# Memory turned by DMA in 2-byte halves instead of by sixteen TensorE transposes, in a two-block transformer kernel

## The reference, cut to what matters

```python
mn = rms_norm_2(mem, norm_mem[l])            # mem: (1, 256, 1024), gain of 1024
xkv = (mn @ xa_w_kv[l]).reshape(b, mem.shape[1], 2, XA_HEADS, XA_HEAD_DIM)
xk = rms_norm_2(xkv[:, :, 0], xa_k_norm[l])
xv = xkv[:, :, 1]
```

## Time and profile before

| | |
|---|---|
| median of 3 runs | 959.49 us (959.39 to 959.93) |
| the profiled execution | 959.49 us, span 957.7 us |
| PE busy | 952.7 us, 99% of the span |
| DVE, ACT, POOL busy | 698.4, 537.6, 125.9 us |
| granted TensorE clock | 1.000 over the whole span |
| HBM traffic | 179 GB/s over the span |

### The profile page before, as it was taken

One profiled execution on the slowest core, in us unless ns is written; L12 is line 12 of the kernel. 1 busy time (PEld: TensorE's weight loads), 2 busy tenths in 40 slices (PEclk: granted clock), 3 DMA queues, 4 the chain that ended last, 5 costly groups with the idle time before them and its releaser, 6 DMA issues.

```text
span 957.7 us, 20451 instructions
## 1 busy us (share of the span) xinstructions
PE 952.7 (99%) x8266; PEld 938.1 (98%) x8266; DVE 698.4 (73%) x1090; ACT 537.6 (56%) x783; POOL 125.9 (13%) x87
## 2 busy tenths in 40 slices
PE   9999999999999999999999999999999999999998
PEld 8999999999999999999999999999999999999998
DVE  5677657477879968877776656688698898887752
ACT  7454454356558964455545465587576674545531
POOL 0111110010036100002111112310002021223100
PEclk9999999999999999999999999999999999999999
DMA  8865675555454454575666665355245355655761
GB/s 264 253 210 176 188 252 167 185 176 179 152 194 140 141 168 133 177 263 176 193 201 198 222 202 178 95 159 175 89 139 172 131 177 174 211 187 177 254 208 65
DMA packets 169167, 172.42 MB, mean 180 GB/s; under 512 B 5748, under 2 KB 167054, under 8 KB 168974
## 3 DMA queue, kind: packets, MB, share of 16 engines
q1 hardware_dynamic: 168270, 170.70, 55.4%
q10 hardware_dynamic: 832, 0.79, 0.3%
HBM read 170.42 MB, written 1.06 MB: 179 GB/s over the span
## 4 chain that ended last, share of the span: by engine, by line
PE 99%; DMA 1%; SPq 0%; DVE 0%; issue 0%; ACT 0%
PE acc L798 87%; PE part L848 1%; PE acc L848 1%; PE part L890 1%; PE part L914 1%; DMA xraw<-in_x 1%; PE part L1204 1%; PE part L900 1%; PE acc L671 1%; PE part L1194 0%; PE part L1227 0%; PE part L1013 0%; PE part L1406 0%; PE part L936 0%; PE part L1214 0%; PE part L1260 0%
## 5 line engine op out<-in xcount | busy, mean ns | idle before, releaser
L464 ACT ACTIVATE wh<-raw 128x1024 fp32r<-128x1024 f32 (+2 forms) x291 | 316.4, 1112 | 269.0 <-PE acc L798 119.2
L483 DVE TENSOR_TENSOR wl<-raw,wh 128x1024 fp32r<-128x1024 f32 (+2 forms) x292 | 393.1, 1385 | 47.2 <-ACT wh L464 46.6
L798 PE MATMUL acc<-ah,wh 128*128 128x256 f32 x1504 | 415.0, 279 | 0.0
L798 PE MATMUL acc<-al,wh 128*128 128x256 f32 x1504 | 409.1, 276 | 0.0
L798 PE MATMUL acc<-ah,wl 128*128 128x256 f32 x1496 | 406.2, 277 | 0.0
L798 PEld LDWEIGHTS acc<-ah,wh 128*128 128x128 f32 x1504 | 282.0, 188 | 3.3 <-issue 2.5
L798 PEld LDWEIGHTS acc<-al,wh 128*128 128x128 f32 x1504 | 280.4, 188 | 0.0
L798 PEld LDWEIGHTS acc<-ah,wl 128*128 128x128 f32 x1496 | 278.0, 188 | 0.1
L798 PE MATMUL acc<-hh,wh 128*128 128x256 f32 x352 | 97.3, 277 | 0.0
L798 PE MATMUL acc<-hh,wl 128*128 128x256 f32 x352 | 97.2, 276 | 0.0
L798 PE MATMUL acc<-hl,wh 128*128 128x256 f32 x352 | 97.2, 276 | 0.0
(11 more groups left out here) (476 smaller groups left out, 1557.2 us busy)
## 6 DMA issues: line engine op xcount, KB each, us to landing
raw<-in_ffn_w_down SPq DMA_DIRECT2D x24, 1408.0 KB, 6.4
raw<-in_w_in SPq DMA_DIRECT2D x33, 1024.0 KB, 5.3
raw<-in_ffn_w_gate SPq DMA_DIRECT2D x32, 1024.0 KB, 5.3
raw<-in_ffn_w_up SPq DMA_DIRECT2D x32, 1024.0 KB, 5.4
raw<-in_w_out SPq DMA_DIRECT2D x8, 1024.0 KB, 5.2
raw<-in_w_proj_attn SPq DMA_DIRECT2D x4, 1024.0 KB, 5.2
raw<-in_w_proj_mlstm SPq DMA_DIRECT2D x4, 1024.0 KB, 5.5
raw<-in_xa_w_kv SPq DMA_DIRECT2D x4, 1024.0 KB, 5.2
```

What stands on the lines that cost most here:

```text
L464: nc.scalar.activation(wh[:, slot, a * nw:b * nw], raw[:, slot, a * nw:b * nw], ACT.Copy).then_inc(S("w_hi"), 1)
L483: nc.vector.tensor_tensor(wl[:, slot, a * nw:b * nw], raw[:, slot, a * nw:b * nw], f(wh[:, slot, a * nw:b * nw]), SUB).then_inc(S("w_lo"), 1)
L798: ins = mm(dst, a, b, start=st and q == 0, stop=en_ and q == sweep[-1], skip_group_check=True)
```

## The change

The memory's transposing leaves TensorE. VectorE copies `memraw` into two planes of 2-byte halves (`mem_planes`: all low halves, all high halves). ScalarE issues four transposing DMAs, one for each half and block of 128 tokens, each over 128 x 1024 elements of two bytes, into `mem_turned`. VectorE then puts the halves together again with two copies, over `memraw`, which now holds `memT` (channels on partitions). `mo` and `mlo` are computed from there instead of from PSUM. The unread 32x256 product after the transposes is gone too. The two new tiles lie in the room of `mo` and `mlo`, which are written later. The diff, without the changes in the list of semaphores:

```diff
@@ sbuf
+        with ExitStack() as sc:
+            mem_planes = sb("mem_planes", [P, 2, TB, D], u16, scope=sc)
+            mem_turned = sb("mem_turned", [P, 2, DC, T], u16, scope=sc)
...
+        mem_halves = memraw[:, :, :].bitcast(u16).rearrange("p b (c h) -> p b h c", h=2)
+        memT = memraw[:, :, :].rearrange("p b c -> p (b c)").rearrange("p (k t) -> p k t", k=DC)
+        memT_halves = memraw[:, :, :].bitcast(u16).rearrange("p b c -> p (b c)").rearrange("p (k t h) -> p h k t", k=DC, h=2)
@@ TensorE
-                                narrow=(1, Q[0]) if (st, q, r) in (("n1", 0, 1), ("n3", 1, 0)) else None)
+                                narrow=(1, Q[0]) if (st, q, r) == ("n1", 0, 1) else None)
...
-            def memory_in(q, r):
-                if (q, r) == (0, 1):
-                    pe.wait_ge(*signal("mem_in", 16))
-                    transpose_in(memraw, "mem_ps", Q[2:6])
-
-            feed_forward("f2u", "f2d", "n3", between=memory_in)
+            feed_forward("f2u", "f2d", "n3")
@@ ScalarE, memory_hi
+                    act.wait_ge(*signal("mem_pl", 1))
+                    for h in range(2):
+                        for b in range(TB):
+                            act.dma_start_transpose(mem_turned[:, h, :, b * P:(b + 1) * P], mem_planes[:, h, b, :]).then_inc(S("mem_tr"), 16)
                 elif q < 3:
+                    act.wait_ge(*signal("mem_T", 1))
                     for j in (2 * q - 2, 2 * q - 1):
-                        act.wait_ge(*signal("mem_ps", j + 1))
                         for c in range(2):
-                            ins = A_(mo[:, 2 * j + c, :], Q[2 + j][:, c * T:(c + 1) * T], ACT.Copy, scale=col(V_MEM + 2 * j + c))
+                            ins = A_(mo[:, 2 * j + c, :], memT[:, 2 * j + c, :], ACT.Copy, scale=col(V_MEM + 2 * j + c))
@@ VectorE, feed_forward and memory_lo
                 looped(dve, FP, body, peel=2 if conv else 1)
+                if st == "n3":
+                    between(-1)
...
-                if q == 0:
+                if q < 0:
+                    dve.wait_ge(*signal("mem_in", 16))
+                    for b in range(TB):
+                        ins = V.tensor_copy(mem_planes[:, :, b, :], mem_halves[:, b, :, :])
+                    ins.then_inc(S("mem_pl"), 1)
+                elif q == 0:
                     dve.wait_ge(*signal("mem_sq", 2))
+                    dve.wait_ge(S("mem_tr"), 64)
+                    for h in range(2):
+                        ins = V.tensor_copy(memT_halves[:, h, :, :], mem_turned[:, h, :, :])
+                    ins.then_inc(S("mem_T"), 1)
                     V.tensor_scalar(e7[:, :], ms7[:, 0:2], EPS, EPS, ADD, MUL).then_inc(S("e7"), 1)
```

More of the change, by code:

```diff
@@ L89, in shared_signals @@
     chains = {
-        "mixer2_dve": [("e7", 1), ("mem_lo", 4), ("kpe", 1), ("la_lo", 1), ("rho2", 1), ("kv_e", 1), ("kv_rd", 1), ("akv", 1),
+        "mixer2_dve": [("mem_pl", 1), ("mem_T", 1), ("e7", 1), ("mem_lo", 4), ("kpe", 1), ("la_lo", 1), ("rho2", 1), ("kv_e", 1), ("kv_rd", 1), ("akv", 1),
                        ("rho7", 1), ("k_ss", 4), ("k_ms", 1), ("eq", 1), ("kt", 1), ("qt", 1), ("gl_cum", 2),
@@ L96, in shared_signals @@
                        ("sog", 1), ("gl_sq", 2), ("gl_sd", 1), ("xf_sd", 1)],
-        "mixer2_pe": [("mem_ps", 4), ("kv_ps", 1), ("uk_ps", 3), ("gl_z", 1), ("uq_ps", 3), ("kq_T", 8),
+        "mixer2_pe": [("kv_ps", 1), ("uk_ps", 3), ("gl_z", 1), ("uq_ps", 3), ("kq_T", 8),
                       ("gl_keT", 1), ("gl_att", 1), ("gl_dS", 3), ("gl_o", 2), ("go_T", 2), ("xq_ss", 2)],
@@ L232, in build @@
         rin = sb("rin", [P, 2, 4])
+        u16 = mybir.dt.uint16
         ah = sb("ah", [P, DC, T], f32r)
@@ L2517, in memory_lo @@
                             k = 2 * j + c
-                            ins = V.scalar_tensor_tensor(mlo[:, k, :], Q[2 + j][:, c * T:(c + 1) * T], col(V_MEM + k), f(mo[:, k, :]), MUL, SUB)
+                            ins = V.scalar_tensor_tensor(mlo[:, k, :], memT[:, k, :], col(V_MEM + k), f(mo[:, k, :]), MUL, SUB)
                         ins.then_inc(S("mem_lo"), 1)
```

## The result

The changed kernel takes 962.97 us (median of 6 runs, 962.49 to 964.73) where the kernel before takes 959.50: a ratio of 1.0037, 95% interval 1.0024 to 1.0050. It is slower by 3.5 us. The time lies in the predicted range, on the predicted side, and 2.0 us above the predicted 961.0.

A forecast was written before the change was run, and what follows sets the result against it. TensorE's stream was taken as the bound (PE busy 952.7 of 957.7 us); from 959.49 us, 1.9 saved and 3.4 waited on ScalarE's issues gave +1.5, 961.0 us, range 957.2 to 975.

The forecast's parts named there:

- What TensorE saves: At slab 2's start, 16 transposes, a slow first step and an unread product leave TensorE: 1.9 us less.
- VectorE's copies: Four copies of 2048 two-byte elements per partition, 1.3 us each; first pair from 558.66 to 561.3, mostly in idle time.
- X: Time of one transposing issue on ScalarE: bounds 0.373 and 2.98 us, middle 1.73 taken.
- The wait on ScalarE: Four issues delay ScalarE's split of slab 2, so TensorE waits 4X - 3.5 us before slab 2: 3.4 us.
- The wait on VectorE: VectorE waits for all four DMAs before its merging copies and slab 3's low part: cost nothing, 0.6 us to spare.
- The sum: TensorE's saving and its wait before slab 2 together: -1.9 + 3.4 = +1.5 us, 961.0 us.
- a fall of the clock: Sign against the forecast: TensorE's granted clock, 1.000 everywhere before, falls behind a wait; no size given.
- All hidden: Rival: X under 0.87 us and DMAs landing in 10 us, leaving only the 1.9 us saving: 957.6 us; 27%.
- Issues of a block each: Rival: each 128x128 block issued as a DMA of its own, X = 2.98 us: 966.0 us; 17%.
- the late landing: Rival: turned data lands at 587.3 in 256-byte packets, TensorE waits 16.3 us before slab 3: 973.9 us; 18%.
- The unread product: 32x256 product behind the transposes at slab 2, counted within the 1.9 us that TensorE saves.

The follow-up runs named there:

- no_dma: Changed kernel without the four transposing DMAs and their waits, VectorE's four copies kept, so the memory isn't turned: 957.94 us, ratio 0.9978.
- two_dma: Changed kernel with only the two transposing DMAs of the low halves, high halves not turned: 957.68 us in the median of ten runs, ratio 0.9987.
- sp_queue: Changed kernel with the four transposing DMAs issued by SyncE, between the loads of slabs 3 and 4, instead of ScalarE: 958.16 us, ratio 0.9981.
- act_behind: Changed kernel with the four transposing DMAs still on ScalarE, but behind its split of slab 2 instead of ahead of it: 963.54 us, ratio 1.0034.
- filled_narrow: Changed kernel with thirty unread 128x256 products ahead of slab 2 and the unread 32x256 product put back behind slab 2's second block: 961.37 us, ratio 1.0022.
- before_no_narrow: Kernel before the change without its unread 32x256 product behind the sixteen transposes, nothing else changed: 962.11 us in the median of eight runs, ratio 1.0018.

## Why the prediction was right, and where it was off
- **What TensorE saves**, 1.9 us: shown. no_dma is 1.95 below before, two_dma 1.94 in the median, and the traces of sp_queue and no_dma gain 1.90 in the stage.
- **VectorE's copies** at 1.3 us each: 1.22 for the planes and 1.32 for the merges, and free (no_dma). The first pair ended at 561.38, predicted 561.3.
- **X**, the time of one issue, taken as the middle of two bounds, 1.73: measured 1.33, 2.10, 1.34 and 2.03, together 6.88 with what lies between them, where I had 6.9. The middle had no reason of its own; that it came out is luck. The estimate from the Trainium skill's page "DMA: Bandwidth & Descriptors", section "Why a DMA increments its semaphore by 16 and not by 1", was 1.5; the mean of the four is 1.70.
- **The wait on ScalarE**, 4X - 3.5 = 3.4 us: 3.3 measured. Shown by taking away its cause in two ways: other queue (sp_queue), half the issues (two_dma).
- **The wait on VectorE**, nothing with 0.6 us to spare: nothing in the changed kernel, where slab 3's first half was ready at 577.85 and TensorE, late and slowed, came for it at 581.00. Where TensorE is in time, in sp_queue, 0.5 us is left. act_behind shows the wait itself: there the last landing came late, as a landing of 571 or later was to do.
- **The sum** was short by 1.6 us. The step that failed is the price of TensorE's wait: the text had it as its length alone, and named a fall of the clock only as something that would make the forecast wrong. By that sign the forecast of +1.5 us was wrong, though the time fell into its wide range. A wait of 3.3 us was followed by 3.4 us at half the clock, 1.6 us more by the rows of the changed kernel, and the same by filled_narrow, where TensorE worked through the wait. The page "TensorE: Matmul & The Clock Gate" of the Trainium skill, section "Part 1: The HAM clock gate (the "warmup" mystery)", says that the clock falls behind an idle stretch; this trace agrees, with 0.50 from 572.61 on, behind an idle stretch of 3.1 us. With 1.6 the sum is +3.1, 962.6, against 962.97; the start of the run can move a time by more than that difference (+0.46 in the profiled one).
- **The rivals.** All hidden was the time that the same change gives from another queue: 957.6 forecast, 958.16 measured beside 959.89. Issues of a block each and the late landing did not come in the changed kernel: the landing took 4.3 us, and eight blocks in one DMA did not go one behind the other at the 1309 ns a block of the Trainium skill's page "VectorE: DVE Perf Modes", section "The three transpose paths", from which the estimate of 42 us was made.
- **The unread product** was counted as a saving of 0.12 us. Here it did no harm to take it out together with the transposes, since the changed kernel, once its clock is back, and sp_queue run at 0.1133 behind the place. Taken out alone it costs 2.5 us in the median of eight runs; the one trace shows 1.6 of it in the stage.

## What to carry to other kernels
A DMA issue holds up the engine that issues it, and a transposing one is here some three to four times as long as a plain one (1.33 to 2.10 us against 0.48): price it as an instruction at its place in that engine's order, and give it to the queue with the most slack, here SyncE. When a wait is added to an engine that never waited, price what follows it too: the clock, and the pace at which it starts again. A product that nobody reads can have a use; before it goes, look at the pitch of the products behind it with and without.

## What the runs showed of the hardware that was not expected
- The same product of 128x256 has two paces at the full clock, 0.1133 and 0.118 us. The slower one can set in behind transposes (6 of 8 runs of before_no_narrow by their times), behind thirty products of another input, or behind a hitch of 0.05 us (two_dma), and then holds for 47 us and more. A product with 32 columns of weights ended it within 0.7 us (filled_narrow).
- The slow pace did not end with the stage. It lasted to 622.1 in two_dma and 624.6 in before_no_narrow, where sums with one output column follow. Behind the same sums the kernel before falls into it as well (0.118 from 622.87 on), so from there on it is no longer ahead by its pace. Over its whole trace the kernel before has 6527 steps of 0.113 to 0.114 us and 818 of 0.117 to 0.119: some 3.7 us of it go to the slow pace. What holds TensorE in it is open.
- Four transposing issues behind each other took 1.33, 2.10, 1.34 and 2.03 us on ScalarE, every second one the longer in either order; the fourth took 3.69 in act_behind. On SyncE they took 1.34, 1.94, 1.31 and 1.38, so there the fourth is short.
- A DMA issue can start before ScalarE's own instruction ahead of it has run (562.17 against 562.31 to 563.57 in act_behind), but ScalarE's next instruction started only when the last issue had ended (570.87 against 570.77).
- VectorE's copies of two-byte elements with a step of two took 1.22 us for 2048, and 1.32 where the step is on the side that is written.
